# Attention of a two-layer decoder: both query blocks of a head in one step, scores biased from PSUM, key norms during the query projection

## The reference, cut to what matters

```python
q = rms_norm(proj[..., :N_HEADS * HEAD_DIM].reshape(B, T, N_KV, GROUP, HEAD_DIM), q_gain)
gates = jax.nn.sigmoid(proj[..., N_HEADS * HEAD_DIM:].astype(f32)).reshape(B, T, N_BRANCH, N_KV, GROUP)
...
s = jnp.einsum('bqgrd,bngd->bgrqn', qi, k_cmp, preferred_element_type=f32) * scale - sl * d_cmp
p_cmp = masked_softmax(s, d_cmp >= 0)
o_cmp = jnp.einsum('bgrqn,bngd->bqgrd', p_cmp, v_cmp.astype(f32))
...
return g[:, :, 0] * o_cmp + g[:, :, 1] * o_slc + g[:, :, 2] * o_win
...
return out @ w_o
```

## Time and profile before

| what | value |
|---|---|
| median of 3 runs | 2596.08 us (2596.07 to 2596.43) |
| span of the profiled execution | 2590.9 us |
| runs' median less that span | 5.2 us |
| TensorE busy | 2513.3 us (97%) |
| VectorE busy | 2152.9 us (83%) |
| mean granted TensorE clock | 0.981 |

### The profile page before, as it was taken

One profiled execution on the slowest core, in us unless ns is written; L12 is line 12 of the kernel. 1 busy time (PEld: TensorE's weight loads), 2 busy tenths in 40 slices (PEclk: granted clock), 3 DMA queues, 4 the chain that ended last, 5 costly groups with the idle time before them and its releaser, 6 DMA issues.

```text
span 2590.9 us, 38545 instructions
## 1 busy us (share of the span) xinstructions
PE 2513.3 (97%) x14006; PEld 2167.4 (84%) x14006; DVE 2152.9 (83%) x2593; ACT 1252.1 (48%) x1654; POOL 376.4 (15%) x205
## 2 busy tenths in 40 slices
PE   6999999998999999999999999899999999999999
PEld 4878888887888888888878788688788888888887
DVE  7899898999999899988998877678989756765666
ACT  4436444535554355435544454573555435543553
POOL 0000110231120012001142200373112001200110
PEclk8999999999999999999999979899999999999999
DMA  9998788986878877887766868207677655555554
GB/s 372 368 377 321 269 329 328 338 326 245 307 283 318 324 285 283 307 330 277 283 247 249 324 250 329 103 1 293 264 287 274 238 186 195 180 193 192 182 178 147
DMA packets 94312, 685.49 MB, mean 265 GB/s; under 512 B 10465, under 2 KB 10465, under 8 KB 11233
## 3 DMA queue, kind: packets, MB, share of 16 engines
q1 hardware_dynamic: 93746, 681.27, 70.1%
q10 hardware_dynamic: 432, 2.38, 0.2%
HBM read 681.51 MB, written 2.10 MB: 264 GB/s over the span
## 4 chain that ended last, share of the span: by engine, by line
PE 78%; DVE 10%; DMA 6%; issue 2%; ACT 2%; POOL 0%; SPq 0%; DVEq 0%; ACTq 0%
PE banks L1518 48%; PE banks L1522 24%; DMA raw<-in_stream 6%; DVE raw L1107 3%; DVE w_lo L1091 3%; ACT w_hi L923 1%; PE banks L779 1%; PE banks L743 1%; PE banks L765 1%; DVE scratch L853 1%; PE banks L782 1%; DVE temp L1175 0%; PE banks L1473 0%; PE banks L1475 0%; PE banks L1476 0%
## 5 line engine op out<-in xcount | busy, mean ns | idle before, releaser
L923 ACT ACTIVATE w_hi<-raw 128x1024 fp32r<-128x1024 f32 x841 | 875.8, 1056 | 990.6 <-PE banks L1522 594.9
L1091 DVE TENSOR_TENSOR w_lo<-raw,w_hi 128x1024 fp32r<-128x1024 f32 x841 | 1089.9, 1318 | 309.9 <-ACT w_hi L923 307.8
L1518 PE MATMUL banks<-h_op,w_hi 128*128 128x512 f32 x3816 | 1203.0, 397 | 6.2 <-DVE w_lo L1091 5.5
L1522 PEld LDWEIGHTS banks<-h_op,w_lo 128*128 128x128 f32 x3816 | 719.0, 188 | 170.0
L1522 PE MATMUL banks<-h_op,w_lo 128*128 128x256 f32 x3816 | 752.1, 278 | 0.0
L1518 PE MATMUL banks<-act_op,w_hi 128*128 128x512 f32 x2176 | 685.8, 397 | 0.6 <-DVE act_op L1252 0.3
L1518 PEld LDWEIGHTS banks<-h_op,w_hi 128*128 128x128 f32 x3816 | 582.4, 189 | 8.4 <-issue 5.8
L1107 DVE CUSTOM_DVE_ANT_0 raw<-raw,c_all 128x2048 f32<-128x2048 f32 x224 | 554.0, 2489 | 15.7 <-ACT c_all L897 9.5
L1522 PEld LDWEIGHTS banks<-act_op,w_lo 128*128 128x128 f32 x2176 | 409.8, 188 | 96.8
L1522 PE MATMUL banks<-act_op,w_lo 128*128 128x256 f32 x2176 | 428.7, 278 | 0.0
L1518 PEld LDWEIGHTS banks<-act_op,w_hi 128*128 128x128 f32 x2176 | 332.1, 189 | 1.8 <-issue 0.9
(11 more groups left out here) (162 smaller groups left out, 1379.7 us busy)
## 6 DMA issues: line engine op xcount, KB each, us to landing
raw<-in_stream SPq DMA_DIRECT2D x645, 1024.0 KB, 5.4
x_res<-in_x SPq DMA_DIRECT2D x1, 2048.0 KB, 11.3
out_x<-x_res SPq DMA_DIRECT2D x4, 512.0 KB, 5.0
mix_area<-in_w_s ACTq DMA_DIRECT2D x1, 1024.0 KB, 9.2
mix_area<-in_b_s ACTq DMA_DIRECT2D x1, 1024.0 KB, 13.8
small<-in_small SPq DMA_DIRECT2D x1, 682.0 KB, 16.3
attn_area<-in_pos ACTq DMA_DIRECT2D x1, 273.0 KB, 5.3
c_all<-in_c SPq DMA_DIRECT2D x1, 8.0 KB
```

Of the source, the lines that this page charges most:

```text
L923: act.activation(w_hi[:, out, 0:n], raw[:, slot, half:half + n], ACT.Copy).then_inc(hi_ready, 1)
L1091: dve.tensor_tensor(w_lo[:, out, 0:n], raw[:, slot, half:half + n], w_hi[:, out, 0:n].bitcast(F32), ALU.subtract).then_inc(stream, 2 if ch ...
L1518: pe.matmul(banks[:, g + j, :], hi[:, k, P * j:P * (j + 1)], operand[:, kt, :], start=(kt == 0), stop=False, skip_group_check=True)
L1522: last = pe.matmul(banks[:, g + j, 0:T], lo[:, k, P * j:P * (j + 1)], operand[:, kt, 0:T], start=False, stop=(kt == last_kt), skip_group_c ...
```

## The change

Every part of the attention is rearranged.

- The loop runs over 16 heads; a step holds both query blocks. The 15 compressed keys stand in front of the selected keys in one array (`k_sel`), so that a block takes two score matmuls instead of three. The scores stay unscaled in PSUM, in bank 5 (block 0) and banks 6 and 7 (block 1), one set for all heads. DVE adds the bias from PSUM in one instruction per block; the query's scale goes into the exponential and the slope.
- A step's eight 128x128 transposes go to banks 0 and 1, one set for all heads; ACT copies bank 0, DVE bank 1. The output of a head, 256 columns, is in bank 4, one for all heads. The compressed values are padded to 128 rows.
- Sums of squares come from matmuls with one column of ones: a 128x128 block of squares is the stationary operand. Those of the keys, the compressed keys and values, and the key norms are made between subpieces of the query chunks 0 and 1 (`keys_pe`, `keys_act`, `keys_dve`); those of the queries and the scores of head 0 stand ahead of the gate matmuls.
- The sigmoid becomes an exponential and a reciprocal. The two `m` of the gate chunk move to query chunks 1 and 2.

```diff
-    "G1": "smmE",
+    "G1": "sE",
...
-            phases.append(("q", [Chunk("q", i, "P3", ("q", 0)) for i in range(4)]))
+            phases.append(("q", [Chunk("q", i, "P4" if i in (1, 2) else "P3", ("q", 0)) for i in range(4)]))
...
+            if place == ("q", 0, 0):
+                pe.wait_ge(keys_squared, 1)
+                for i in range(16):
+                    last = pe.matmul(banks[:, 2, i:i + 1], key_squares[:, P * i:P * (i + 1)], ones[:, 0:1],
+                                     start=True, stop=True, skip_group_check=True)
+                last.then_inc(key_sums, 1)
...
+        def query_sums_pe(pe, chunks):
+
+            for i in chunks:
+                pe.wait_ge(queries_squared, i + 1)
+                for n in range(2 * TPC):
+                    j = 2 * TPC * i + n
+                    last = pe.matmul(banks[:, 7, 480 + j:481 + j], squares[:, P * j:P * (j + 1)], ones[:, 0:1],
+                                     start=True, stop=True, skip_group_check=True)
+            last.then_inc(query_sums, 1)
...
+        def score_pe(pe, h):
+
+            g = h // GRP
+            if h:
+                pe.wait_ge(biased, 2 * h)
...
+        def attention_pe(pe):
+
+            for i in range(NH + 3):
+                if i + 1 < NH:
...
+                    score_pe(pe, i + 1)
...
+                h = i - 2
+                if 0 <= h < NH:
+                    pe.wait_ge(weights_scaled, h + 1)
+                    if h:
+                        pe.wait_ge(short_read, h)
+                        pe.wait_ge(long_read, h)
+                    at = 0
+                    for qb in range(2):
+                        for o in [0] + list(range(16, ROW[qb], P)):
+                            last = pe.transpose(flat_pt[:, at:at + P], row(h, qb)[:, o:o + P], ident[:, :])
...
+                h = i - 3
+                if h >= 0:
+                    g = h // GRP
+                    pe.wait_ge(short_read, h + 1)
+                    pe.wait_ge(long_read, h + 1)
+                    if h:
+                        pe.wait_ge(out_lo, h)
...
+                    last.then_inc(pv_done, 1)
...
         def attention_act(act):
...
+                h = i - 2
+                if 0 <= h < NH:
+                    act.wait_ge(turned, 2 * h + 1)
...
+                    act.activation(probs_t(h)[:, 0:4 * P], banks[:, 0, :], ACT.Copy).then_inc(short_read, 1)
+                h = i - 3
+                if h >= 0:
+                    act.wait_ge(pv_done, h + 1)
+                    act.activation(act_op[:, h, 0:T], banks[:, 4, 0:T], ACT.Copy).then_inc(out_hi, 1)
...
         def attention_dve(dve):
...
+            for i in range(NH + 4):
+                if i < NH:
...
+                    for qb in range(2):
+                        dve.wait_ge(scored, 2 * i + qb + 1)
+                        dve.scalar_tensor_tensor(
+                            out=row(i, qb), in0=pos[:, ROW[0] * qb:ROW[0] * qb + ROW[qb]],
+                            scalar=slope_q[:, 2 * i + qb:2 * i + qb + 1],
+                            in1=flat_long if qb else banks[:, 5, 0:ROW[0]], op0=ALU.mult, op1=ALU.add) \
+                            .then_inc(biased, 1)
+                h = i - 4
+                if h >= 0:
+                    dve.wait_ge(out_hi, h + 1)
+                    dve.tensor_tensor(act_op[:, h, T:HILO], banks[:, 4, 0:T], act_op[:, h, 0:T].bitcast(F32),
+                                      ALU.subtract).then_inc(out_lo, 1)
+                if i < NH:
+                    dve.wait_ge(biased, 2 * i + 2)
+                    for qb in range(2):
+                        dve.tensor_reduce(by_row(neg_max, i)[:, qb, 1:3],
...
+                h = i - 1
+                if 0 <= h < NH:
+                    d, f = denom[:, 6 * h:6 * h + 6], coef[:, 6 * h:6 * h + 6]
+                    dve.wait_ge(exp_ready, h + 1)
...
+                h = i - 3
+                if 0 <= h < NH:
+                    dve.wait_ge(turned, 2 * h + 2)
+                    if h >= 2:
+                        dve.wait_ge(pv_done, h - 1)
+                    dve.tensor_copy(probs_t(h)[:, 4 * P:8 * P], banks[:, 1, :]).then_inc(long_read, 1)
...
+                if name == "gate":
+                    query_sums_pe(pe, range(3))
+                    score_pe(pe, 0)
+                    query_sums_pe(pe, (3,))
```

More of the change, by code:

```diff
@@ L73 @@
 N_SMALL = C_W2 + 2 * HD
-DW = 16 + T
-N_POS = 2 * DW + 2
+KEYS = (P, 2 * P)
+ROW = tuple(16 + 2 * n for n in KEYS)
+PAIR = sum(ROW)
+POS_SLOPE = PAIR
+POS_SEEN = PAIR + 2 * NH
+N_POS = POS_SEEN + 2
+KSC = 16 + T
+RING = 4
 PAT = {
@@ L289, in build @@
     n_pieces = TOTAL["G"] if stop is None else BY_NAME[stop][0].n["G"]
-    slopes = [2.0 ** (-8.0 * (h + 1) / NH) for h in range(NH)]
     ctx = ExitStack()
@@ new lines, in build @@
+        gates_t = area[0:NGATE, 7680:7680 + T]
+        stats = temp[:, 1, 0:512]
+        neg_max, denom, coef = (stats[:, 96 * i:96 * (i + 1)] for i in range(3))
+        rms_q, inv_q, slope_q = (stats[:, 288 + 32 * i:320 + 32 * i] for i in range(3))
+        k_gains = vstat[:, 0:3]
+        r_k = vstat[:, 4:20]
+        sq_c, r_c = rstd[:, 0:NB], rstd[:, 64:64 + NB]
+        flat_pt = banks[:, 0:2, :].rearrange("p a t -> p (a t)")
+        flat_long = banks[:, 6:8, :].rearrange("p a t -> p (a t)")[:, 512 - KSC:512 + T]
@@ new lines, in scores, with row, probs_t, by_row @@
+        def scores(h):
+            return temp[:, 0, 0:PAIR] if h == 0 else area[:, PAIR * (h % RING):PAIR * (h % RING + 1)]
+        def row(h, qb):
+            return scores(h)[:, ROW[0] * qb:ROW[0] * qb + ROW[qb]]
+        def probs_t(h):
+            return area[:, 3328 + 1024 * (h % 2):3328 + 1024 * (h % 2 + 1)]
+        def by_row(ap, h):
+            return ap[:, 6 * h:6 * h + 6].rearrange("p (q b) -> p q b", q=2)
+        def compressed(h):
+            return scores(h)[:, 0:2 * ROW[0]].rearrange("p (q k) -> p q k", q=2)[:, :, 0:NCMP]
@@ L980, in evacuate @@
                 g = group(prev)
-                if e == 0 and kind in ("ua", "uv", "u", "kvf", "q", "cmp", "gate"):
+                if e == 0 and kind in ("ua", "uv", "u", "kvf", "q", "cmp"):
                     done_wait(act, prev)
@@ L984, in evacuate @@
                         out, src = cmp_g[:, :].rearrange("p (i n) -> p i n", i=2), banks[:, g:g + 2, NB:2 * NB]
-                    elif kind == "gate":
-                        out, src = gates_t, banks[0:NGATE, g, T:HILO]
                     else:
@@ L1016, in evacuate @@
                     act.activation(cmp_g[:, :], cmp_g[:, :], ACT.Gelu_apprx_tanh).then_inc(cmp_gelu, 1)
-                if e == 2 and kind == "cmp":
-                    act.activation(squares[:, 4096:6144], scratch[:, 4096:6144], ACT.Square).then_inc(keys_squared, 1)
                 if e == 2 and kind == "q":
@@ L1224, in evacuate @@
                         out, src = cmp_g[:, :].rearrange("p (i n) -> p i n", i=2), banks[:, g:g + 2, 0:NB]
-                    elif kind == "gate":
-                        out, src = gates_t, banks[0:NGATE, g, 0:T]
                     else:
```

485 lines of the change are left out of this document (219 added, 266 removed).

## The result

The changed kernel takes **2611.93 us** (median of four, 2606.97 to 2612.52) against 2596.07 for the kernel before on the same chip: ratio 1.0061, 95% interval 1.0047 to 1.0075, or +15.9 us. The forecast was +24, 2620 us.

A forecast was written before the change was run, and what follows sets the result against it. PE was taken as near its limit, busy 97% of the span. Full-clock change +4.1, loop clock +12, start +3, last turns +3, one-column sums +2: +24, span 2615, plus 5.2 makes 2620 us; range 2595 to 2637.

The forecast's parts named there:

- the 5.2 us put on top of the span: Whole kernel: runs take 5.2 us over the profiled span, so a span of 2615 becomes 2620 us.
- The ring: Attention loop: bank 1 copy, transposes, value products, output copy, low part, maxima, next copy; 6.25 us per head against 5.25.
- The signs named for it: Loop timeline: VectorE idle about 2 us before low part, transposes waiting for bank 1 copy, POOL idle 2 us or more.
- The clock in the loop: Attention loop: PE idle 2 us per turn lets the granted clock fall; 7.35 us per head, +12 over eleven turns.
- Half the time at each level: Attention loop: clock half at 1.00 (turn 6.25 us), half at 0.50 (turn 8.9 us), giving 7.35 per head.
- The one-column sums: Chunk 0 and prelude: one-column matmuls may let the clock fall; +2 us, bounds 0 and +7.
- The moved key work: Query chunk 0: 8.5 us of PE work moved from the prelude, gaining nothing by itself since PE is full.
- Ring open, faster: Rival, attention loop: output copy is there when VectorE arrives, turn 4.5 us by POOL plus slack; 2577 us, chance 0.12.
- The value beside it: Same rival's variant, attention loop: POOL's 4.26 shrinks without SBUF blocking, turn towards PE's 4.05; about 2572 us.
- Clock at 1.00: Rival, attention loop: the clock stays at 1.00; 2602 us, chance 0.20.
- clock at 0.50 throughout: Rival, whole loop: clock stays at 0.50, eleven turns at 8.9 us, +29 instead of +12; 2638 us, chance 0.12.
- it changes little: Rival, attention loop: a turn costs only 5.5 to 5.9 us; about 2594 us, chance 0.06.

The follow-up runs named there:

- Experiments 1 to 3: Changed kernel with bank 1 copy earlier, 2589.27 us; value products before transposes, 2588.58; dummy VectorE addition before the output-copy wait, 2612.63, or behind the low part, 2613.28.
- experiment 4: Changed kernel with the sums of squares of keys and queries streaming 128 columns of ones instead of one: 2604.92 us, ratio 1.0040 to the kernel before.
- the kernel with the low part late: Changed kernel with VectorE's copy of bank 1 directly behind the bias and the output's low part moved behind maxima and coefficients: 2576.50 us, ratio 0.9913.
- early copy: Changed kernel with VectorE's copy of bank 1 moved ahead of the output's low part, directly behind the bias: 2589.27 us, ratio 0.9984 to the kernel before.

## Why the prediction was right, and where it was not

The call, slower by over 0.2%, and the range were right; the time was 8 us too high. Of these, 3 lie outside the sum of the stages: the 5.2 us put on top of the span came from one profiled execution that was faster than its kernel's median, and in the changed kernel the median is only 2.1 us over the span. The other 5 are in the stages.

**The ring was right**, with its place and its price. Copy to transposes 0.15 (forecast 0.15); transposes and products to ACT's start 2.88 (2.87 and 0.04); output copy to low part 0.42 (0.50: the sum took L569's 468 ns for a plain copy, which takes 384); low part to end of the next copy 2.74 (2.70). Together 6.19 against 6.25. The signs named for it are all there: idle time of 2.37 us before the low part, transposes released by the copy of bank 1 and not by POOL, POOL idle 2.58. Experiments 1 to 3 show it: opened, shortened, and padded inside and outside.

**The clock in the loop was right in kind and too large.** It fell, as reasoned from the earlier trace rows, but in three of eleven turns and not half of the time, and a slow turn costs 1.64 us and not 2.65. The mean turn was 6.64 instead of 7.35: +5 us in place of +12. The step that failed is "Half the time at each level": from one fall no share follows. For the start +3 was forecast, as if it went at 0.50; it went at 0.91 (1657.67 to 1676.97) and took 19.3 us where 24 stood. The end took 19.1 of a forecast 19.2.

**The one-column sums were mis-sized.** The sum had +2 with bounds 0 and +7. Measured: 22.06 us of prelude where 14.05 stood, and 10.1 for the chunks where 8.5 stood, +9.6 together, beyond the bound. The prelude's price at full clock was right, as experiment 4 shows (13.9 us to the start of the last gate matmul, 14.2 to its end). The upper bound was too low, since it had the gate matmuls and some subpieces at half rate but not the sums themselves: L661 takes 11.6 us instead of 7.2, the gate matmuls 7.9 instead of 5.5, the scores of head 0 2.7 instead of 1.35. And the value inside the bounds was badly chosen: the row nearest in columns, from the earlier trace rows, was the right one, and the sum went less than a third of the way to it.

**The moved key work was right**: nothing is gained by moving it where PE is full. No gap of PE opened in the chunks, and the modulation pieces cost nothing that shows. Over all four chunks PE is busy 101.93 of 101.93 us. A window over one chunk's length in which they came has VectorE at 19.20 us (forecast 19.5) and the transfers at 371 GB/s (forecast 376), and PE full at 1.00:

```profile
1579.20:1601.40 22.20, 22.20 (x129) 19.36 (x129) 19.20 (x18) 9.06 (x9) 0.00 (x0) 1.00 0.95 371
```

The forecast left out that the output projection starts at full clock, since the attention now ends at 1.00: 2.0 us.

So two errors partly cancel: by spans the chunks and the prelude came out 7.6 us over the forecast with its +2, the start and the loop 12.5 under it, and the 1.75 ahead of the chunks and the 2.0 behind the attention went unforecast. That the time lands within 8 us is in part luck.

**The rivals.** "Ring open, faster" failed for this kernel: the ring is closed. Its price was near what the kernel with the low part late shows, though not for its own reasons: it said 4.5 per turn by POOL and 2577 us, and that kernel runs at PE's 4.02 and 2576.50 us, the shorter turns being offset in the main by a prelude that costs 8 us more than the rival had. The value beside it (PE's 4.05, 2572) had the turn right. Of POOL's shrinking, which was named there, the runs show as much: POOL takes 3.62 us per head instead of 4.26 (its 256-column scalings 929 ns on the mean, before 1080), and the dummy addition with two SBUF inputs lengthened a POOL instruction by 270 ns. The Trainium skill (SBUF — State Buffer, Who interferes with whom) says that such a VectorE instruction contends with a GpSimd instruction that reads SBUF; the trace agrees, but POOL was not on the ring, so it gave no time. That the 4.26 shrank for this reason alone was not tried. "Clock at 1.00" (2602) fell by the slow turns; "clock at 0.50 throughout" (2638; its own terms add up to 2637) by their small number; "it changes little" by the turn, 6.19 us and not 5.5 to 5.9.

## What to carry to other kernels

When buffers are halved, write down for each engine what stands in its queue behind the wait that frees them, and follow the chain until it comes back to its start: if it returns within one turn, its length is a lower bound of the period, however idle the engines are. The cure need not be another buffer; here two blocks of one engine's step changed places, which took the turn from 6.19 to 4.02 us. After opening a ring, look for the next one (5.45 us here, through ACT) before believing a bound by work; and keep matmuls wide and PE's pauses short, since here both a pause of 2 us in each turn and a run of one-column matmuls were paid a second time in the clock.

## What the runs showed of the hardware that was not expected

- A run of one-column matmuls, each with a weight load of 128 columns, without a gap on PE, let the granted clock fall to 0.50 (0.78 from 1635 to 1640, 0.50 from 1640 to 1650), and the matmuls after it ran at half rate too. Streaming 128 columns instead kept it at 1.00 (in all three profiles) and took 7.5 us instead of 11.6. In two of the nine profiles with one-column query sums the first 48 kept full rate (5.4 and 5.7 us for them, elsewhere 7.1 to 8.2).
- Slow turns came with PE's idle time per turn, but not in its order: none of 11 turns at up to 1.1 us, 3 to 5 of 11 at 2.0, one of 11 at 2.6, four of 11 at 3.2. The Trainium skill (TensorE: Matmul & The Clock Gate, Why this matters for your kernels) asks for no long pause between bursts of matmuls; these traces show falls with pauses of 2.0 us that come every 6.2 us.
- The exponential of 256 elements takes 586 ns with a scale from SBUF and 508 without; those of 128 elements 478 against 402. The cause was not tried by itself.
- Kernels that are the same up to the query projection reach it at 1529.1 to 1537.1 us, in one profiled execution each. The runs of a single kernel spread as far (early copy: 2583.69 to 2596.08), so this need not be a difference between the kernels. A difference of a few us between medians here isn't yet a cause.
